# Splitting row blocks and their sums once, ahead of the seven products

## The reference

```python
h_lat = layer_norm(x) * (1.0 + sc_l[:, None, :]) + sh_l[:, None, :]
q, k, v, o, z, g = jnp.split(h @ w_in, ODD_SPLITS, axis=-1)   # w_in: 1024 x (5 * 1024 + 16)
```

## Time and profile before

| | |
|---|---|
| median of 3 runs | 3592.77 us (3590.75 to 3596.95) |
| profiled execution | 3590.2 us, its span 3588.4 us |
| TensorE busy | 3368.0 us (94%) |
| VectorE, ScalarE, GpSimd busy | 2363.6, 1358.4, 1776.7 us |
| part of queries and sums | 2057 to 2284 us |
| part of the seven products | 2284 to 2976 us |

### The profile page before, as it was taken

One profiled execution on the slowest core, in us unless ns is written; L12 is line 12 of the kernel. 1 busy time (PEld: TensorE's weight loads), 2 busy tenths in 40 slices (PEclk: granted clock), 3 DMA queues, 4 the chain that ended last, 5 costly groups with the idle time before them and its releaser, 6 DMA issues. The chain is left out here.

```text
span 3588.4 us, 49705 instructions
## 1 busy us (share of the span) xinstructions
PE 3368.0 (94%) x16176; PEld 2479.7 (69%) x16176; DVE 2363.6 (66%) x3529; ACT 1358.4 (38%) x2274; POOL 1776.7 (50%) x1214
## 2 busy tenths in 40 slices
PE   7999997799999999999889799799999998999798
PEld 5788885455555555555478699687878786877587
DVE  4666544778877777777767654466565645777566
ACT  3433335444444444444420133234343423654200
POOL 1033213477777777777634334322566313444354
PEclk8999998899999999999999999999999999999899
DMA  5335545411111111111245455565545446777563
GB/s 205 112 111 140 139 144 173 163 33 36 36 36 35 36 36 35 36 36 35 94 153 185 160 171 179 194 200 157 170 137 171 157 154 205 221 223 240 188 228 135
DMA packets 358834, 475.36 MB, mean 132 GB/s; under 512 B 57933, under 2 KB 212445, under 8 KB 358513
## 3 DMA queue, kind: packets, MB, share of 16 engines
q1 hardware_dynamic: 300592, 358.80, 32.0%
q10 hardware_dynamic: 51600, 94.16, 8.5%
q0 software_dynamic: 6448, 19.94, 1.4%
HBM read 337.32 MB, written 135.36 MB: 132 GB/s over the span
## 5 line engine op out<-in xcount | busy, mean ns | idle before, releaser
L2410 DVE TENSOR_REDUCE al_mx<-al_sx 128x1 f32<-128x512 f32 (+1 forms) x960 | 559.1, 631 | 201.8 <-PE al_sx L2513 192.1
L2330 ACT ACTIVATE al_e<-al_st 128x1024 f32<-128x1024 f32 x432 | 443.2, 1027 | 535.4 <-PE al_st L2528 535.3
L2379 POOL TENSOR_TENSOR al_acc_p<-al_acc_p,al_e 128x1024 f32<-128x1024 f32 x188 | 455.7, 2424 | 19.8 <-POOL al_acc_p L2379 0.9
L319 PE MATMUL pb_acc<-p_whi,pb_r_hi 128*128 128x512 f32 x952 | 375.7, 395 | 34.4 <-DVE pb_r_lo L1765 23.7
L2537 PE MATMUL al_acc<-al_e,vres 128*64 128x512 f32 x1728 | 402.5, 601 | 0.0
L321 PE MATMUL pb_acc<-p_whi,pb_r_lo 128*128 128x512 f32 x952 | 372.8, 392 | 0.0
L320 PE MATMUL pb_acc<-p_wlo,pb_r_hi 128*128 128x512 f32 x952 | 372.5, 391 | 0.0
L2527 PE MATMUL al_st<-al_qa,kres 128*128 128x512 f32 x864 | 346.4, 401 | 3.8 <-issue 3.2
L2528 PE MATMUL al_st<-al_qb,kres 128*128 128x512 f32 x864 | 341.1, 395 | 0.0
L1765 DVE TENSOR_TENSOR pb_r_lo<-pb_stg,pb_r_hi 128x512 fp32r<-128x512 f32 x238 | 218.2, 918 | 168.5 <-ACT pb_r_hi L1665 164.5
L2513 PE MATMUL al_sx<-kres,al_qx 128*128 128x512 f32 (+1 forms) x960 | 310.4, 396 | 9.6 <-DVE al_mx L2410 7.5
(11 more groups left out here) (340 smaller groups left out, 7413.2 us busy)
## 6 DMA issues: line engine op xcount, KB each, us to landing
pb_stg<-s_hsum ACTq DMA_DIRECT2D x238, 256.0 KB, 2.7
s_proj<-pb_out SPq DMA_DIRECT2D x72, 256.0 KB, 3.2
p_wst<-in_w1s ACTq DMA_DIRECT2D x18, 1024.0 KB, 5.4
ml_k<-s_proj SPq DMA_DIRECT2D x36, 512.0 KB, 4.4
ml_v<-s_proj SPq DMA_DIRECT2D x36, 512.0 KB, 8.9
hm_w<-in_ada_w SPq DMA_DIRECT2D x16, 1024.0 KB, 7.8
ml_qt<-s_qt SPq DMA_DIRECT2D x32, 512.0 KB, 6.4
s_h<-ml_h POOLq DMA_DIRECT2D x32, 512.0 KB, 8.3
```

Of the source, the lines that this page charges most:

```text
L319: nc.tensor.matmul(out, s_hi, m_hi, start=start, stop=False)
L2330: nc.scalar.activation(e[:, pair(p, j), :, :], st[(NP * p + j) % 2][:, :, 0:W], ACT.Exp).then_inc(e_done, 1)
L2379: nc.gpsimd.tensor_tensor(acc_p[:], acc_p[:], e[:, pair(p, j)], ALU.add).then_inc(add_p, 1)
L2410: V.tensor_reduce(mx[:, x:x + 1], slots[x % NSX][:, 0:spans[x % NS][1]], AX.X, ALU.max).then_inc(sx_max, 1)
```

## The change

The row blocks and sums are split in the first part, and both parts of each are stored (`s_hsum` has twice the size); the second part loads both and splits nothing.

In the first part the three blocks of rows are stored from `pa_h_hi` and `pa_h_lo` (which the last pair now has too) and no longer from `pa_ht`, so that the ring waits for these stores and `pa_ht` no longer does. GpSimd's third and fourth sums change places; the four sums lie in three places (0, 1, 2, 0). For each sum there is a high part on ScalarE (`sum_high`) and a low part in place on VectorE (`sum_low`). SP stores a sum when its low part is made.

In the second part the loads are of 512 KB into a ring of six; TensorE waits for the load alone. The low parts of weights 4 and 5 of group 0 move from GpSimd to VectorE, and all weight work of the start ahead of the products' own work there.

```diff
-    sums = m.sb(tag + "sums", [P, 2, 4, P])
+    sums, sum_hi = m.sb(tag + "sums", [P, 3, 4, P], F32R), m.sb(tag + "sum_hi", [P, 2, 4, P], F32R)
...
+    SUM_ORDER, PLACE = (0, 1, 3, 2), (0, 1, 2, 0)
...
     def slot_free(eng, i):
...
-            eng.wait_ge(row_stored, 32 * pair + 32)
-            if pair < LAT:
-                eng.wait_ge(hi_done, i - NH + 1)
-                eng.wait_ge(lo_done, i - NH + 1)
+            eng.wait_ge(hi_done, i - NH + 1)
+            eng.wait_ge(lo_done, i - NH + 1)
+
+    def split_free(eng, i):
+        if i >= RING:
+            eng.wait_ge(mm_done, 4 * ((i - RING) // 2 + 1))
+            eng.wait_ge(row_stored, 64 * ((i - RING) // 2 + 1))
...
             def rows(pair):
-                modulated(sp, 2 * pair)
                 view = s["hsum"][pair]
...
+                for i in (2 * pair, 2 * pair + 1):
+                    for part, (done, t) in enumerate(((hi_done, h_hi), (lo_done, h_lo))):
+                        sp.wait_ge(done, i + 1)
+                        if i % 2 == 0:
+                            sp.dma_start(view[0:2, :, part].rearrange("o p f -> p o f"), t[:, i % RING].rearrange("p (o k) n -> p o (k n)", o=2).bitcast(F32)).then_inc(row_stored, 16)
+                        else:
+                            sp.dma_start(view[2, :, part], t[:, i % RING, 4:KD].rearrange("p k n -> p (k n)").bitcast(F32)).then_inc(row_stored, 16)
+
+            def sum_out(pair, q):
+                sp.wait_ge(sum_lo_done, 4 * pair + q + 1)
+                view = s["hsum"][pair, 3 + SUM_ORDER[q]]
+                for part, t in enumerate((sum_hi[:, q % 2], sums[:, PLACE[q]])):
+                    sp.dma_start(view[:, part], t.rearrange("p k n -> p (k n)").bitcast(F32)).then_inc(sum_stored[q], 16)
...
+            def sum_high(pair, q):
+                act.wait_ge(sum_done, 4 * pair + q + 1)
+                if q >= 2:
+                    act.wait_ge(sum_stored[q - 2], 32 * pair + 32)
+                elif pair:
+                    act.wait_ge(sum_stored[q + 2], 32 * pair)
+                nc.scalar.activation(sum_hi[:, q % 2], sums[:, PLACE[q]].bitcast(F32), ACT.Copy).then_inc(sum_hi_done, 1)
...
                     if i < NT:
                         modulate(i)
-                        if i < 2 * LAT:
-                            high(i)
+                        high(i)
+                    sum_high(pair, b)
                 for b in range(2):
                     gate_out(2 * pair + b)
                     if q:
                         query_out(4 * pair + 2 + b)
+                    sum_high(pair, 2 + b)
...
+                terms = ((a21, a22, ALU.add), (place[0], a11, ALU.subtract), (a12, place[1], ALU.subtract), (a11, a21, ALU.subtract))
+                for q, (x, y, op) in enumerate(terms):
+                    if q == 3:
+                        pool.wait_ge(sum_stored[0], 32 * pair + 32)
+                    elif pair:
+                        pool.wait_ge(sum_stored[(3, 1, 2)[q]], 32 * pair)
+                    if q:
+                        pool.wait_ge(sum_done, 4 * pair + q)
+                    G.tensor_tensor(place[PLACE[q]], x, y, op).then_inc(sum_done, 1)
...
+            def sum_low(pair, q):
+                dve.wait_ge(sum_hi_done, 4 * pair + q + 1)
+                if q < 2:
+                    dve.wait_ge(sum_done, 4 * pair + q + 2)
+                place = sums[:, PLACE[q]]
+                V.tensor_tensor(place, place.bitcast(F32), sum_hi[:, q % 2].bitcast(F32), ALU.subtract).then_inc(sum_lo_done, 1)
...
                     if i < NT:
                         modulate(i)
-                        if i < 2 * LAT:
-                            low(i)
+                        low(i)
+                    sum_low(pair, i % 2)
                 for i in (2 * pair + 4, 2 * pair + 5):
                     if i < NT:
                         w.normalised(dve, i)
+                    sum_low(pair, 2 + i % 2)
...
 def seven_products(nc, m, s, keep, w, cols, dec):
 
-    tag, NSTG, RING = "pb_", 4, 4
+    tag, RING = "pb_", 6
...
             def load(g):
...
-                act.dma_start(stg[:, g % NSTG].rearrange("p k n -> p (k n)"), s["hsum"][UNITS[u][1], w.ROWS[i]]).then_inc(ld[g % NSTG], 16)
-
-            def high(g):
-                act.wait_ge(ld[g % NSTG], 16 * (g // NSTG) + 16)
                 if g >= RING:
                     act.wait_ge(mm_done, g - RING + 1)
-                nc.scalar.activation(r_hi[:, g % RING], stg[:, g % NSTG], ACT.Copy).then_inc(hi_done, 1)
+                act.dma_start(rows[:, g % RING].rearrange("p w k n -> p w (k n)").bitcast(F32), s["hsum"][UNITS[u][1], w.ROWS[i]]).then_inc(ld[g % RING], 16)
...
-                if j in (0, 2, 3):
-                    w.w_high(act, (0, {0: 4, 2: 6, 3: 5}[j]))
+                if j in (0, 1):
+                    w.w_high(act, (0, (6, 5)[j]))
...
-                if j in (0, 3):
-                    w.w_low(G, (0, 5 if j else 4))
...
-            for g in range(2):
-                low(g)
             w.w_low(V, (0, 3))
-            for g in range(2, RING):
-                low(g)
+            w.w_low(V, (0, 4))
+            w.w_add(V, 0, 5)
+            w.w_low(V, (0, 6))
+            w.w_low(V, (0, 5))
...
-                if j + RING < N:
-                    low(j + RING)
...
-                pe.wait_ge(lo_done, j + 1)
+                pe.wait_ge(ld[j % RING], 16 * (j // RING) + 16)
...
-        "hsum": dram("s_hsum", (NT // 2, 7, P, CH)),
+        "hsum": dram("s_hsum", (NT // 2, 7, P, 2, CH)),
```

More of the change, by code:

```diff
@@ L1390, in _ @@
                 sp.wait_ge(g_stored[i], 16 * PAIRS)
-                sp.wait_ge(sum_stored[i], 32 * PAIRS)
-            sp.wait_ge(row_stored, 32 * PAIRS)
+            for q in range(4):
+                sp.wait_ge(sum_stored[q], 32 * PAIRS)
+            sp.wait_ge(row_stored, 64 * PAIRS)
         @block.scalar
@@ L1406, in high @@
                 modulated(act, i)
[L1407 to L1408 removed]
+                split_free(act, i)
                 nc.scalar.activation(h_hi[:, i % RING], ht[:, i % NH], ACT.Copy).then_inc(hi_done, 1)
@@ L1461, in row_sums @@
                 a11, a12, a21, a22 = ta[:, 0:4], ta[:, 4:KD], tb[:, 0:4], tb[:, 4:KD]
[L1462 to L1468, removed]
+                place = [sums[:, n].bitcast(F32) for n in range(3)]
+                terms = ((a21, a22, ALU.add), (place[0], a11, ALU.subtract), (a12, place[1], ALU.subtract), (a11, a21, ALU.subtract))
[7 more added lines that the diff above has]
+                    G.tensor_tensor(place[PLACE[q]], x, y, op).then_inc(sum_done, 1)
             w.inverse_deviation(pool, 2)
@@ L1585, in seven_products @@
     turn = [sum(gated[:u]) for u in range(NU)]
-    stg = m.sb(tag + "stg", [P, NSTG, 4, P])
-    r_hi, r_lo = m.sb(tag + "r_hi", [P, RING, 4, P], F32R), m.sb(tag + "r_lo", [P, RING, 4, P], F32R)
+    rows = m.sb(tag + "rows", [P, RING, 2, 4, P], F32R)
     s1, s5, u2, t5 = (m.sb(tag + n, [P, CH]) for n in ("s1", "s5", "u2", "t5"))
@@ L1672, in sigmoid @@
                 nc.scalar.activation(sg[:, at % 2], out[:, kind], ACT.Sigmoid).then_inc(sg_done[kind], 1)
-            for g in range(NSTG):
+            for g in range(RING):
                 load(g)
-            for g in range(2):
-                high(g)
             w.w_high(act, (0, 3))
-            for g in range(2, RING):
-                high(g)
-            for g in range(NSTG, NSTG + RING - 1):
-                load(g)
+            w.w_high(act, (0, 4))
             for j in range(N):
@@ L1693, in _ @@
                     nc.scalar.activation(s5[:], acc[j % BANKS][:], ACT.Copy).then_inc(s5_done, 1)
-                if j + RING < N:
-                    high(j + RING)
                 if i == 5 and gated[u]:
@@ L1761, in _ @@
             V = nc.vector
-            def low(g):
-                dve.wait_ge(hi_done, g + 1)
-                V.tensor_tensor(r_lo[:, g % RING], stg[:, g % NSTG], r_hi[:, g % RING].bitcast(F32), ALU.subtract).then_inc(lo_done, 1)
-            for g in range(2):
-                low(g)
             w.w_low(V, (0, 3))
-            for g in range(2, RING):
-                low(g)
+            w.w_low(V, (0, 4))
+            w.w_add(V, 0, 5)
+            w.w_low(V, (0, 6))
+            w.w_low(V, (0, 5))
             for j in range(N):
@@ L1834, in _ @@
                 for k in range(4):
-                    mm = split_mm(nc, acc[j % BANKS][:], r_hi[:, j % RING, k, :], r_lo[:, j % RING, k, :],
+                    mm = split_mm(nc, acc[j % BANKS][:], rows[:, j % RING, 0, k, :], rows[:, j % RING, 1, k, :],
                                   w.whi[i][:, k, :], w.wlo[i][:, k, :], k == 0, k == 3)
```

22 lines of the change are left out of this document (5 added, 17 removed).

## The result

The changed kernel takes 3650.48 us (median of 4 runs, 3649.40 to 3670.47). The kernel before took 3591.76 us beside it (4 runs, 3590.67 to 3596.95). The ratio is 1.0169 with an interval of 1.0135 to 1.0202: slower, as forecast, and 6.5 us above the number forecast. The profiled run of after took 3651.38 us, its span 3649.6.

The account below looks back on a forecast made before the run. The first part was taken to run at TensorE's pace until a chain of waits slows it: 57.4 us there, 14.8 at its end, minus 18.5 in the products, +53.7 on 3590.2 gives 3644 us, range 3610 to 3668.

Parts of the forecast that it names:

- The loop, +6.3 us a pair: First part: chained waits of x loads behind low parts make a pair 32.5 us against TensorE's 26.2; plus 57 us.
- three legs: First part's loop: second to third low part 10.1 us, third to fourth 10.1, fourth to the next second 12.3.
- One sign: First part, profile after: VectorE should wait for x at its statistics, some 4 to 5 us each.
- the extra work of pairs 3 and 5: First part: weight work after these pairs makes the next second low part 5.6 and 6.7 us later.
- my plain leg: First part: from a pair's fourth low part to the next pair's second, without weight work, 12.3 us.
- The end of the part: From the last query step to the products' first load: a chain of 19.1 us, now 4.3; plus 15 us.
- The products: Seven products: waits at the start and at the weights' changes shrink, doubled reads cost nothing; minus 18.5 us.
- The weights' changes: Seven products: the three waits of 15.8 us in all fall to 0.7 us each; minus 13.5 us.
- The start: Seven products: product 5 starts 26.5 us after the boundary and not 31.8; minus 5 us (0 to 9).
- That of collisions: First part: GpSimd's third sum goes before VectorE's low part, six loops 1.3 us longer; 3652 us, chance 0.16.
- The rival of transfers: Seven products: doubled reads beside stores and weights make them bound by transfers, +8 us; 3652 us, chance 0.06.
- The rival of "not slower": First part stays at TensorE's pace, loop under 26.2 us; 3586.5 us, chance 0.12.

Follow-up runs that it names:

- Both loads of x ahead: Against the changed kernel, SP issues the loads of x for tiles 2p+4 and 2p+5 before the second and third sums' stores; 3600.80 us, ratio 1.0025.
- the versions with weights ahead: Weights 3 split and weights 6 loaded at the first part's end, on both early x loads, with or without last-pair reordering and turned sum places; 3600.88 and 3596.49 us.
- GpSimd's subtraction late: GpSimd's weight subtraction moved behind the last pair's sums, on both early x loads, with or without last-pair reordering and turned sum places; 3598.00 and 3598.88 us.
- the products alone: Second part as changed, first part as before but storing each unsplit block twice, so output is not the reference's; 3585.13 us, ratio 0.9972 against the kernel before.
- the turning places: Against the changed kernel, sums take the three places in turn, so a pair's first sum waits for the previous second sum's store; 3654.26 us, ratio 1.017.

## Why the prediction was right

**The loop, +6.3 us a pair, right.** From the fourth low part of pair 0 to that of pair 6 it takes 210.6 us; forecast 207.3 (six times 32.5, and 5.6 and 6.7). The loops take 31.7 to 37.4 us each (forecast 32.5 to 39.2). By their three legs, summed over the six loops: second to third low part 62.2 us (forecast 60.6), third to fourth 66.5 (60.6), fourth to the next second 81.9 (86.1). The last query copy comes at 2341.5, forecast 2337.3. Both loads of x ahead brings 58 of 60 us back, so that it is this loop is shown and not only argued. One sign was read off wrongly: I had VectorE wait 4 to 5 us for each x, and it waited 6.1 on average (84.9 us in 14), which is what my own terms give, 1.4 of issues and 4.7 of landing.

**Its terms were less right than their sum.** So that the sum came within 3.3 us is in part luck. From 2093 to 2300 us x lands at a median of 4.0 us where I took 4.7, and the sums' stores at 2.8 (high parts) and 3.4 (low parts) where I took 3.9. Why is open: the DMA share is 0.54 in both stretches, and with both loads of x ahead, at a share of 0.72, x lands in 4.2, so emptier queues don't explain it. Against that stand single late landings (VectorE's longest wait for x is 8.1 us). By the page of the Trainium skill on DMA: Bandwidth & Descriptors (Anatomy of one DMA), whose fit is for GpSimd's queue, x would land in 3.2 us, as an estimate; the shortest landing in the whole trace is 3.5, so here the trace decides, against it.

**Pair 2 was missed, 4 us.** GpSimd's low part of weights after that pair meets the normalisation, which takes 4.97 us:

```profile
2173.62 4.50 POOL L1253 TENSOR_TENSOR p_wlo<-p_wst,p_whi 128x2048 fp32r<-128x2048 f32 x1
```

It begins 0.08 us before VectorE's row of 2173.70, shown above. I had that pair of rows as the earlier trace rows, but used it only for a rival. I listed the extra work of pairs 3 and 5 and not that of pair 2. With it the forecast of the fourth low part of pair 6 goes from 2319.6 to 2323.8; it ended at 2323.2. The Trainium skill (SBUF — State Buffer, Who interferes with whom) has it that the engine which issues first keeps a pair of ports shared by the two for its whole instruction. The rows agree: GpSimd's began first, and VectorE's ended 0.5 us behind it.

**Pair 3 cost 3.9 and not 5.6 beyond my plain leg, pair 5 6.4 and not 6.7** (16.2 and 18.7 us from the fourth low part on, against the 12.3 that I had). Three of the four plain legs measured are 11.2 us, one is 13.3; beyond those three the two pairs cost 5.0 and 7.5. After pair 3 GpSimd's first sum starts sooner than I had it, and its second takes 3.40 us beside VectorE's low part of weights:

```profile
2216.59 1.30 POOL L1490 TENSOR_TENSOR pa_sums<-pa_ht 128x512 f32<-128x512 f32 x1 [0.58 <-DMA s_hsum<-pa_sums]
2218.04 3.40 POOL L1490 TENSOR_TENSOR pa_sums<-pa_sums,pa_ht 128x512 f32<-128x512 f32 x1
```

**The end of the part, 20.8 us, forecast 19.1.** The chain was as written, up to the fourth sum of the last pair, at 2353.13, 11.6 us after the last query copy (forecast 12.8). The high part of it then stood behind a copy of gates that waited for the store of earlier gates, a wait that I had not listed:

```profile
2356.07 0.37 ACT L1433 ACTIVATE pa_gst<-pa_gacc,pa_gbias 128x128 f32<-128x128 f32 x1 [2.30 <-DMA s_graw<-pa_gst]
2356.34 0.62 ACT L1441 ACTIVATE pa_sum_hi<-pa_sums 128x512 fp32r<-128x512 f32 x1
```

**The products, -19.9, forecast -18.5.** The weights' changes gave 13.8 us (15.8 less 2.0), forecast 13.5. The start gave 3.5, where I had 5: product 5 is 28.2 us after the first load and not 26.5. The step that was mis-sized is the weights' landing. I had the weight in the middle of the queue decide, through VectorE's subtraction of it (2378.52 to 2380.81). It was the last one, whose load lands some 21.6 us after the boundary:

```profile
2383.93 1.91 ACT L1248 ACTIVATE p_whi<-p_wst 128x2048 fp32r<-128x2048 f32 x1 [10.35 <-DMA p_wst<-in_w1s]
```

Behind it come one high part and two low parts, which end at 2390.4. The 2.6 us left over of the 19.9 are not accounted for by waits; TensorE's busy time over the part is 1.8 us less (658.6 from 660.4), for no reason shown. That the sum came within 1.4 us of the forecast says little: in the eight traces that have this second part unchanged it takes 669.3 to 677.3 us, with 0 to 5.3 us of waits at the changes of weights.

**The rivals.** That of collisions was half right: they happen, but not where I had put them. At the second sum's end VectorE's low part of the first sum comes first by some 0.04 us and takes 0.69, and it is GpSimd's third sum that pays (1.77 to 1.81 us, not 1.29). What VectorE loses is its low part of the second sum beside GpSimd's fourth, as in pair 1:

```profile
2124.06 1.76 DVE L1529 TENSOR_TENSOR pa_sums<-pa_sums,pa_sum_hi 128x512 fp32r<-128x512 f32 x1
...
2123.66 1.62 POOL L1490 TENSOR_TENSOR pa_sums<-pa_ht 128x512 f32<-128x512 f32 x1 [2.02 <-DMA s_hsum<-pa_sums]
```

That is 1.1 us in four of the seven pairs (0, 1, 4 and 6). It is also the case that I had meant with the page: a VectorE instruction with two large inputs. The row that I had set beside it has one. With the 4.2 of pair 2, and 2 us in each of pairs 3 and 5 (the last normalisation and the fourth low part, beside a subtraction of weights), the collisions made at least 12 us. In the sum the shorter landings paid for most of them. The rival of transfers is refuted for the running products, where TensorE never waits for a row block behind the first, even in a stretch fuller than any before:

```profile
2440.00:2480.00 40.00, 40.00 (x177) 32.93 (x176) 12.15 (x23) 4.47 (x7) 12.81 (x11) 1.00 0.93 324
```

At the start of the products what the versions with weights ahead showed fits it. The rival of "not slower" is what both loads of x ahead makes of the kernel: within 0.25% of before. In my terms that version should have given 3586.5. It gave 3600.8, though its gain in the products (18.8 us in its trace) and its end (+16.1) are the forecast's within 1.3 us. What remains is 2.4 us in the first part, some 2.3 behind the products, and a first query copy 8.6 us later than in the profile of before.

That last difference is not the change's work. It arises 1400 us ahead of it, where all the kernels are the same line for line. The products `hm_acc`, which begin at 592 to 594 us in both traces, end at 679.5 us and not at 672.0, and the clock that TensorE was granted there is 0.77 and not 1.00 (columns as in the earlier trace rows; before, then both loads of x ahead):

```profile
620.00:680.00 60.00, 48.69 (x350) 31.48 (x349) 54.13 (x146) 42.36 (x221) 47.85 (x66) 1.00 0.75 245
620.00:680.00 60.00, 55.06 (x310) 35.86 (x302) 45.73 (x123) 37.16 (x199) 44.10 (x62) 0.77 0.71 234
```

Six traces have 0.94 to 1.00 there and their first query copy between 2077.6 and 2081.2 us; four (both loads ahead, the first with weights ahead, both with GpSimd's subtraction late) have 0.77 to 0.84 and theirs between 2086.4 and 2087.5. The eleventh, of the products alone, has 0.89 and 2073.4; it reached `hm_acc` 3.6 us before any other. Why the clock was lower in some executions is open, and so is whether some versions meet it more often. Until that is known, differences of up to 9 us between single profiles, and small ones between medians, are no measure of what an edit of the second projection does.

No version that computes the reference is faster than before; for four of them the interval of the ratio includes 1. The kernel that leaves the splitting out gained 0.28% (0.15 to 0.41), which shows about what there was to win in this arrangement.

## What to carry to other kernels

When a store in an in-order queue gets a new wait, list what is issued behind it, a load above all. Here two loads of x behind a low part cost 58 us, while 72 new instructions and twice the stores cost the running part some 2. Before work is moved out of a part in which it is hidden, read how much of it TensorE waits for: 34 us of waits was all that could be gained from 476 instructions. A loop of waits can't be shortened by striking one of its terms without asking what then runs beside the others; the turning places show it. Before two profiles are compared by their whole spans, look at where they differ ahead of the first changed line: here it was up to 9 us, with the granted clock beside it.

## What the runs showed of the hardware

In this kernel neither a DMA share of 0.7 nor one of 0.93 was a limit: TensorE was busy throughout in the row above (324 GB/s). In the first 5 us of the products (granted clock 0.50, its lower level) it reached

```profile
2367.00:2372.00 5.00, 4.90 (x12) 3.84 (x13) 2.29 (x1) 1.40 (x2) 0.00 (x0) 0.50 1.03 408
```

408 GB/s, where the share of before scaled up had given 343.

The issue of a transfer takes SP's queue time that depends on more than its size. In the version with GpSimd's subtraction late, the two issues of the 512 KB row blocks (L1343) take 0.51 and 0.47 us at the median over the nine pairs, and those of the 256 KB blocks right behind them (L1345) 1.08 and 0.97. Why the smaller ones take longer was not tried.

What VectorE and GpSimd cost each other depends on which began first: a normalisation of 0.81 us took 4.97 beside a weight's low part of 4.50 and 1.78 beside a sum of 1.31; and GpSimd's second sum, 1.29 alone, took 3.40 beside VectorE's low part of 2.29. In the last case VectorE began 0.04 us sooner, and it is GpSimd that pays. VectorE's normalisation reads one large operand; its low part reads two, and it too took 1.76 and not 0.69 beside a sum.
